# The first layer's expert matmuls, ordered in blocks of latent passes and of context passes

## What is computed

```python
def expert_choice_ffn(h, w_router, w_gate, w_up, w_down):
    bsz, n, _ = h.shape
    cap = CAPACITY_FACTOR * n // N_EXPERTS
    aff = jax.nn.softmax(jnp.einsum('bnd,de->bne', h, w_router).astype(jnp.float32), axis=-1)
    g, idx = lax.top_k(aff.transpose(0, 2, 1), cap)
    ...
    xs = h[bidx, idx]
    hid = jax.nn.silu(jnp.einsum('becd,edf->becf', xs, w_gate)) * jnp.einsum('becd,edf->becf', xs, w_up)
    y = jnp.einsum('becf,efd->becd', hid, w_down) * g[..., None].astype(h.dtype)
    return jnp.zeros_like(h).at[bidx, idx].add(y)
```

## Time and profile before

| | |
|---|---|
| median of 3 runs | 2340.63 us |
| lowest, highest | 2337.3, 2345.62 us |
| the profiled execution: its own time | 2342.0 us |
| the profiled execution: its span | 2340.2 us |
| mean granted TensorE clock over it | 0.946 |
| TensorE busy | 2032.5 us, 87% |

### The profile page before, as it was taken

How to read it: one execution, slowest core, us unless ns; L and a number is a source line. 1 busy time by engine, 2 the same in 40 slices (tenths; PEclk the granted TensorE clock), 3 DMA queues, 4 the chain that set the end, 5 groups by cost and what they waited for, 6 DMA issues and landing times.

```text
span 2340.2 us, 24430 instructions
## 1 busy us (share of the span) xinstructions
PE 2032.5 (87%) x9884; PEld 873.8 (37%) x9884; DVE 709.1 (30%) x1506; ACT 519.6 (22%) x1081; POOL 82.9 (4%) x128
## 2 busy tenths in 40 slices
PE   5998978989669999999999969896888598888885
PEld 3555545654312222222222235454553132222231
DVE  1023566761430210211112050257852311111113
ACT  4131134432311111111101151313432111111111
POOL 0000000000100000000000000000001000000000
PEclk9999979999879999999999989997999799999997
DMA  8111046541659779779778611101014799999994
GB/s 365 37 72 37 36 149 227 200 177 49 245 204 358 292 277 359 276 292 360 276 291 308 240 66 65 43 0 30 17 37 166 306 428 428 428 428 427 429 428 195
DMA packets 46489, 529.38 MB, mean 226 GB/s; under 512 B 5664, under 2 KB 5920, under 8 KB 16976
## 3 DMA queue, kind: packets, MB, share of 16 engines
q1 hardware_dynamic: 34400, 486.72, 52.8%
q0 software_dynamic: 11872, 41.62, 4.8%
q10 hardware_dynamic: 144, 0.01, 0.0%
HBM read 513.65 MB, written 14.68 MB: 226 GB/s over the span
## 4 chain that ended last, share of the span: by engine, by line
PE 65%; DMA 17%; DVE 12%; ACT 3%; issue 2%; SPq 0%; POOL 0%; DVEq 0%; ACTq 0%; POOLq 0%
DMA ring<-in_wstream 16%; PE ps L1468 14%; PE ps L1212 9%; PE ps L1378 6%; PE ps L1502 6%; PE ps L1472 5%; PE ps L1190 5%; PE ps L1507 3%; PE ps L1432 2%; PE ps L1136 2%; PE ps L1304 1%; DVE work L898 1%; PE ps L1322 1%; PE ps L1182 1%; PE ps L1160 1%
## 5 line engine op out<-in xcount | busy, mean ns | idle before, releaser
L1468 PE MATMUL ps<-ring,work 128*64 128x512 f32 x2048 | 483.1, 608 | 39.2 <-DMA ring<-in_wstream 34.7
L1064 DVE TENSOR_TENSOR work<-glao,ps 128x512 f32<-128x512 f32 x32 | 22.0, 687 | 910.0 <-ACT glao L607 910.0
L1468 PEld LDWEIGHTS ps<-ring,work 128*64 128x64 f32 x2048 | 134.4, 138 | 379.3 <-issue 316.2
L1502 PE MATMUL ps<-big,work 128*64 128x512 f32 x1024 | 240.5, 607 | 4.2 <-ACT work L613 3.1
L1212 PE MATMUL ps<-hT,ring 128*128 128x512 f32 (+1 forms) x592 | 206.4, 507 | 1.9 <-DVE hT L735 1.4
L1212 PEld LDWEIGHTS ps<-hT,ring 128*128 128x128 f32 x592 | 112.2, 190 | 95.0 <-issue 86.4
L607 ACT ACTIVATE glao<-ps 128x512 f32<-128x512 f32 x32 | 19.1, 597 | 564.4 <-PE ps L1472 324.3
L1378 PE MATMUL ps<-ring,hT 128*128 128x512 f32 x320 | 138.6, 595 | 0.0
L1472 PE MATMUL ps<-ring,work 128*32 128x512 f32 x1024 | 136.4, 605 | 0.0
L1432 PE MATMUL ps<-work 128*128 128x512 f32 x256 | 119.5, 604 | 12.4 <-DVE hT L1095 9.9
L1502 PEld LDWEIGHTS ps<-big,work 128*64 128x64 f32 x1024 | 67.0, 137 | 160.5 <-issue 149.7
(11 more groups left out here) (236 smaller groups left out, 1965.9 us busy)
## 6 DMA issues: line engine op xcount, KB each, us to landing
ring<-in_wstream SPq DMA_DIRECT2D x166, 2048.0 KB, 8.5
big<-in_wstream SPq DMA_DIRECT2D x64, 2048.0 KB, 10.2
x_kept<-big POOLq DMA_DIRECT2D x14, 512.0 KB, 2.9
big<-x_kept POOLq DMA_DIRECT2D x14, 512.0 KB, 7.5
xn_lat<-big POOLq DMA_DIRECT2D x8, 512.0 KB, 16.6
big<-in_x_all SPq DMA_DIRECT2D x6, 512.0 KB, 6.5
work<-in_nat_bias POOLq DMA_DIRECT2D x16, 192.0 KB, 2.6
big<-in_x_all POOLq DMA_DIRECT2D x6, 512.0 KB, 9.5
```

The source lines that it names most:

```text
L1468: last = T.matmul(bank(m)[64 * h:64 * h + 64, :], XST[:, kc, e, 0:CAP_L], gate_up[j][:, kk, m * D + h * 512:m * D + (h + 1) * 512], start= ...
L1502: last = T.matmul(bank(3)[64 * g:64 * g + 64, :], HT[:, kc, 0:CAP_L], down[kc // 4][:, kc % 4, h * 512:(h + 1) * 512], start=kc == 0, stop ...
```

## The change

The matmuls and their operands are the same ones; their order within a unit of weights is another, in the first layer only. Within a unit, all the context's matmuls stand together and all the latents', and which of the two comes first alternates from unit to unit: in the up part the context first in units 0 and 2 and the latents first in units 1 and 3, in the down part the latents first in unit 0 and the context first in unit 1. `ffn_full[j]` is waited for once at a unit's start as before, and `ffn_used[j]` is raised behind the unit's last matmul. With `ctx_too` false the order stays what it was. The new lines are L1467 and L1475 (up: latents, context) and L1516 and L1524 (down: latents, context).

```diff
-                    for j in range(4):
-                        pe.wait_ge(ffn_full[j], i * 32 + 16 * (e + 1 + l * NE))
+                    def up_lat(j):
                         for kk in range(2):
                             kc = 2 * j + kk
                             for m in range(2):
                                 for h in range(2):
                                     last = T.matmul(bank(m)[64 * h:64 * h + 64, :], XST[:, kc, e, 0:CAP_L],
                                                     gate_up[j][:, kk, m * D + h * 512:m * D + (h + 1) * 512], start=kc == 0, stop=kc == KC - 1)
-                            if ctx_too:
-                                for g in range(4):
-                                    last = T.matmul(bank(2)[32 * g:32 * g + 32, :], XST[:, kc, e, CAP_L:CW],
-                                                    gate_up[j][:, kk, g * 512:(g + 1) * 512], start=kc == 0, stop=kc == KC - 1)
+                        return last
+
+                    def up_ctx(j):
+                        for kk in range(2):
+                            kc = 2 * j + kk
+                            for g in range(4):
+                                last = T.matmul(bank(2)[32 * g:32 * g + 32, :], XST[:, kc, e, CAP_L:CW],
+                                                gate_up[j][:, kk, g * 512:(g + 1) * 512], start=kc == 0, stop=kc == KC - 1)
+                        return last
+
+                    for j in range(4):
+                        pe.wait_ge(ffn_full[j], i * 32 + 16 * (e + 1 + l * NE))
+                        if not ctx_too:
+                            last = up_lat(j)
+                        elif j % 2:
+                            up_lat(j)
+                            last = up_ctx(j)
+                        else:
+                            up_ctx(j)
+                            last = up_lat(j)
                         last.then_inc(ffn_used[j], 1)
...
+                    def down_lat(j):
+                        for kc in range(4 * j, 4 * j + 4):
+                            for g in range(2):
+                                h = g ^ e
+                                last = T.matmul(bank(3)[64 * g:64 * g + 64, :], HT[:, kc, 0:CAP_L],
+                                                down[j][:, kc % 4, h * 512:(h + 1) * 512], start=kc == 0, stop=kc == KC - 1)
+                        return last
+
+                    def down_ctx(j):
+                        for kc in (4 * j, 4 * j + 2):
                             for g in range(4):
-                                h, k = (g // 2) ^ e, kc - 1 + g % 2
+                                h, k = (g // 2) ^ e, kc + g % 2
                                 last = T.matmul(bank(4)[32 * g:32 * g + 32, :], HT[:, k, CAP_L:CW],
-                                                down[k // 4][:, k % 4, h * 512:(h + 1) * 512], start=kc == 1, stop=kc == KC - 1)
-                        if kc % 4 == 3:
-                            last.then_inc(ffn_used[4 + kc // 4], 1)
+                                                down[j][:, k % 4, h * 512:(h + 1) * 512], start=kc == 0, stop=kc == KC - 2)
+                        return last
+
+                    for j in range(2):
+                        pe.wait_ge(ffn_full[4 + j], i * 32 + 16 * (e + 1 + l * NE))
+                        if not ctx_too:
+                            last = down_lat(j)
+                        elif j:
+                            down_ctx(j)
+                            last = down_lat(j)
+                        else:
+                            down_lat(j)
+                            last = down_ctx(j)
+                        last.then_inc(ffn_used[4 + j], 1)
```

## The result

The change took the time from a median of 2341.27 us (four runs, 2337.3 to 2345.62) to **2305.23 us** (four runs, 2304.0 to 2307.6): the ratio is 0.9847, with a 95% interval of 0.9827 to 0.9866. Forecast were 2304, between 2297 and 2311.

What follows compares the result with a forecast made beforehand. PE's own passes were taken to bound the first layer's experts; 8 merged blocks of each kind at 0.289 us, over 16 experts, save 37.0 us. From 2342.0 that leaves 2305.0, forecast as 2304 us, range 2297 to 2311.

Steps and rivals of the forecast that it cites:

- The bound: First layer's experts: only how fast PE's own passes follow each other sets the length; PE busy 643.55 of 656 us.
- The 0.289 us a round: First layer's experts: a latent plus a context block takes 2.863 us, 0.289 over six bare passes, for changing tile width.
- The count: Per expert, 12 latent and 12 context blocks become 4 and 4: 2.31 us saved, 37.0 us for 16 experts.
- The edges: Where up and down parts meet, within and between experts: one change of width either way, so no cost or gain.
- The joins at 0.43 us: Passes inside merged blocks follow at 0.43 us, no extra; upper bound 0.02 each for context joins, 2.6 us in all.
- both rivals on bare loads: At merged joins: weight loads lie bare, 2338 us, chance 0.02; or the context's four loads queue up, 2371, chance 0.02.
- The sum: Whole kernel: profiled execution 2342.0 less 37.0 is 2305.0 us, span 2303.2; the runs' median 1.4 lower, stated as 2304.
- The prediction's list of signs: What the changed profile would show: up part 21.3 us, down part 10.7, joins 0.43, stage about 618, no transfer waits.
- The 19 us to spare: First layer's weight slots: at least 21 us between a load's landing and its use before, some 19 after the change.

Runs made afterwards that it cites:

- e4: Kernel before, order kept, with the first layer's 64-column latent tiles split into two of 32 columns; 2290.14 us, ratio 0.9781.
- e6: Changed kernel with the first layer's latent tiles split into 32 columns as in e4; 2288.62 us, ratio 0.9779 to the kernel before.
- e1: Changed kernel with the down part's old alternating loop put back, so only the up part is reordered; 2311.78 us, ratio 0.9878 to before.
- e2: Changed kernel with the up part's old alternating loop put back, so only the down part is reordered; 2329.75 us, ratio 0.9949 to before.
- e5: Changed kernel, first layer's up part running all four units' latents, then all their context, releasing slots late; 2296.07 us, ratio 0.9803 to before.

## Why the prediction was right

*The bound.* PE's own passes set the length of the first layer's experts. The stage's waits stayed the same to 0.1 us, and everything taken from between the passes came off the time.

*The 0.289 us a round.* It was costed from the long rows, split as 0.15 and 0.14. The changed kernel's blocks of 16 and of 8 passes show the same extras, and e4 shows a round at 2.57 us, without them. That they come with the change of width was argued in the prediction from joins in other stages; e4 and e6 show it. What they don't part is the width of a tile from the number of tiles side by side, since 64 columns always came in twos here and 32 in fours.

*The count.* Eight blocks of each kind an expert, 2.31 us, so 4.62 a pair: measured 4.61. The edges were said to cost nothing either way. e1 and e2 show why that had to be counted: each part by itself gains at the edge what the other gives back.

*The joins at 0.43 us.* Taken at no extra, with 0.02 as the upper bound for the context's. The rows of the changed kernel have 0.43 at each, so both rivals on bare loads are out. The Trainium skill's page "TensorE: Matmul & The Clock Gate", section "Part 3: Packing small matmuls — row/col tiling", lets, in its list of what overlaps, a weight load overlap only with matmuls on other rows of the array; the rows here, with all 128 rows in use and the loads hidden, disagree, and the measurement decides. Its paragraph above that list also lets a load into the background weight buffer be pulled ahead, which the hidden loads would fit, though no row tells which buffer a load goes to. On the change of width itself the Trainium skill's page "TensorEngine Tiling (Array Packing)", section "Key Properties", says that changing the tiling mode drains TensorE. The trace has a delay at each such place, 0.53 to 0.55 us to the next block where a pass takes 0.43, which would fit a drain. It shows one thing more there: the new width's loads start only with the new block. Whether the delay is a drain, or is these loads lying bare, no run parts; the prediction's price holds either way, and the cause below the width stays open.

*The sum.* The profiled spans differ by 2340.2 - 2302.8 = 37.4 us, the medians by 36.0; forecast were 37.0. The 37.4 isn't quite the same 37.0, though, and the agreement is in part luck. From the experts' first matmul to the first of L1368 behind them, the stage took 1339.71 - 666.00 = 673.71 us before and 1302.49 - 667.34 = 635.15 after: 38.56 less. Of these, 1.64 us aren't the change's. In the kernel before, the first latent block of the very last down part ran largely at the lower of the two clock levels (1.2 GHz), after PE had waited 1.44 us for DVE and 0.52 us for nothing that the profile names; in the changed kernel the same place ran at the higher one (2.4 GHz), with the same two waits ahead of it. The windows over that last down part, 0.91 of the full clock before and 1.00 after:

```profile
1322.00:1340.00 18.00, 14.76 (x73) 4.09 (x74) 3.47 (x6) 3.34 (x6) 2.23 (x5) 0.91 0.97 409
```

```profile
1287.00:1302.50 15.50, 12.13 (x73) 4.11 (x73) 3.61 (x6) 3.46 (x7) 1.96 (x4) 1.00 0.98 402
```

PE's timeline at the stage's start and at that place, before and then after:

```profile
666.00 3.41 PE L1468 MATMUL ps<-ring,work 128*64 128x512 f32 x8 [2.32 <-issue]
...
1322.13 0.66 PE L1440 MATMUL ps<-cst,work 128*128 128x128 f32 x4 [1.44 <-DVE work L1064]
...
1324.03 3.40 PE L1502 MATMUL ps<-big,work 128*64 128x512 f32 x8 [0.52 <-issue]
1327.36 1.25 PE L1507 MATMUL ps<-big,work 128*32 128x512 f32 x8
1328.54 1.94 PE L1502 MATMUL ps<-big,work 128*64 128x512 f32 x8
...
1339.71 3.70 PE L1368 MATMUL ps<-work,ones 128*128 128x512 f32 x8 [2.52 <-ACT work L627]
```

```profile
667.34 3.38 PE L1475 MATMUL ps<-ring,work 128*32 128x512 f32 x16 [2.32 <-issue]
...
1287.28 0.66 PE L1440 MATMUL ps<-cst,work 128*128 128x128 f32 x4 [1.44 <-DVE work L1064]
...
1289.18 3.65 PE L1516 MATMUL ps<-big,work 128*64 128x512 f32 x16 [0.52 <-issue]
1292.76 3.64 PE L1524 MATMUL ps<-big,work 128*32 128x512 f32 x32
...
1302.49 3.70 PE L1368 MATMUL ps<-work,ones 128*128 128x512 f32 x8 [2.50 <-ACT work L627]
```

The block of 8 records at 1324.03 takes 3.33 us to its successor where the ordinary one takes 1.87, and the context block behind it 1.18 for 1.00: 1.64 us in all, which the changed kernel happened not to pay. What is left, 38.56 - 1.64 = 36.92 us, is the change's own part and meets the 37.0. The part of the program ahead of the experts, which the change doesn't touch, was 1.34 us longer (667.34 for 666.00), and the part behind them 0.18 us shorter, which makes the 37.4. Such shifts were in the range, not in the sum.

*Two slips.* The prediction's list of signs gave a latent block of the up part as eight passes in 3.6 us. It is sixteen in 7.0; eight in 3.6 is the down part's. The sum did not use it. And a load was said to land in 7.7 us afterwards as well; it is 9.8 in the changed kernel's stage:

```profile
ring<-in_wstream SPq DMA_DIRECT2D x60, 2048.0 KB, 9.8
```

The 19 us to spare were thus more like 17. They were enough: PE waited for no transfer in the changed kernel's stage, nor in e5's, where a load took 13.6 us.

## What to carry to other kernels

Where tiles of two widths alternate on TensorE and nothing else holds it up, count the changes of width and price them: here 0.15 us for each 64-column block and 0.14 for each 32-column one, together 16 x 12 x 0.289 = 55 us, a twelfth of this stage before. Grouping by width takes back what the grouping allows and no more, and each join at a group's edge counts, so write out the sequence over the loop's end too. Better still is to cut the wide operand into tiles of the narrow width, if it fills the array as well: it left no change of width within an expert's up and down parts, needed no reordering, and the 1,536 more matmul records that it executed cost nothing that could be measured (2290 us against the change's 2305).

## What the runs showed of the hardware that was not expected

A 2 MB load's time to land grew with the pace at which the loads were asked for, while the stage's mean rate was well under the 428 GB/s of the earlier trace rows: 7.7 us from issue at 297 GB/s, 9.8 at 314, and 13.6 in e5 at 317, when four were issued within 5.46 us. So it isn't the mean rate that sets it: in one such burst of e5 the four loads landed 7.6, 10.8, 14.0 and 17.2 us after their issue, each later than the one ahead of it. A pass of two 64-column tiles and one of four 32-column tiles take the same 0.429 us, so twice the number of matmuls for the same columns was free. The second pass after a change comes late by 0.05 us among 64-column tiles and by 0.02 among 32-column ones, so even the restart is cheaper with the narrow ones.
